# Two fewer plain pairs in FFNs 2 to 4 of a float32 decoder trunk on one Trainium2 core

## The reference, cut to what matters

```python
def modulate(x, g, shift, scale):
    return rmsnorm(x, g) * (1.0 + scale[:, None, :]) + shift[:, None, :]

def swiglu(h, w13, w2):
    gate, up = jnp.split(h @ w13, 2, axis=-1)
    return (jax.nn.silu(gate) * up) @ w2
...
        h = modulate(x, norm_g[i, 0], ada[:, 0, 0], ada[:, 0, 1])
        x = x + 0.5 * ada[:, 0, 2, None, :] * swiglu(h, ffn_w13[i, 0], ffn_w2[i, 0])
        ... (mixer 0: mLSTM, mixer 1: differential attention)
        h = modulate(x, norm_g[i, 2], ada[:, 2, 0], ada[:, 2, 1])
        x = x + 0.5 * ada[:, 2, 2, None, :] * swiglu(h, ffn_w13[i, 1], ffn_w2[i, 1])
```

## Time and profile before

| | |
|---|---|
| median of 3 runs | 1879.09 us (1878.94 to 1879.1) |
| the profiled execution, device time | 1878.92 us |
| its span in the trace | 1877.1 us |
| PE busy | 1858.1 us, 99% of the span |
| PE weight loads | 1679.9 us, 89% |
| DVE busy | 1457.2 us, 78% |
| ACT busy | 890.2 us, 47% |
| POOL busy | 41.5 us, 2% |
| DMA | 270.87 MB, 144 GB/s on average |

### The profile page before, as it was taken

The page is one execution under the profiler, slowest core; times in us unless marked ns, Lnnn a source line. Parts: engine busy times, 40 slices in busy tenths (PEclk is TensorE's granted clock), DMA queues, the critical chain, the costliest instruction groups (busy, mean ns, idle before and its releaser), DMA issues. The chain is left out here.

```text
span 1877.1 us, 30566 instructions
## 1 busy us (share of the span) xinstructions
PE 1858.1 (99%) x11872; PEld 1679.9 (89%) x11872; DVE 1457.2 (78%) x2041; ACT 890.2 (47%) x1414; POOL 41.5 (2%) x36
## 2 busy tenths in 40 slices
PE   8999999999999999999999999999999999999998
PEld 6999988888779999998899999889877799999887
DVE  7899978785678888878688887886787778888433
ACT  6566632344334656642255655224344555656322
POOL 4000000000000100000010000000000010000000
PEclk9999999999999999999999999999999999999999
DMA  8344369624113422359643232972321243322432
GB/s 316 120 161 163 110 242 332 237 92 157 57 46 124 135 104 98 112 215 334 212 146 106 108 112 87 349 246 82 113 68 45 72 131 113 112 100 96 138 99 83
DMA packets 84115, 270.87 MB, mean 144 GB/s; under 512 B 8593, under 2 KB 16913, under 8 KB 83258
## 3 DMA queue, kind: packets, MB, share of 16 engines
q1 hardware_dynamic: 83616, 267.62, 41.5%
q0 software_dynamic: 352, 2.11, 0.3%
q10 hardware_dynamic: 58, 0.00, 0.0%
HBM read 261.30 MB, written 8.40 MB: 144 GB/s over the span
## 5 line engine op out<-in xcount | busy, mean ns | idle before, releaser
L698 PE MATMUL acc<-h_hi,w_hi 128*128 128x256 f32 (+1 forms) x1178 | 378.6, 321 | 4.1 <-DVE w_lo L1765 1.2
L1975 DVE TENSOR_TENSOR w_lo<-arena,w_hi 128x1024 fp32r<-128x1024 f32 (+1 forms) x288 | 307.5, 1088 | 95.7 <-ACT w_hi L1333 92.8
L1256 ACT ACTIVATE w_hi<-arena 128x1024 fp32r<-128x1024 f32 (+2 forms) x223 | 201.4, 904 | 369.0 <-DMA arena<-w 174.3
L700 PE MATMUL acc<-h_hi,w_lo 128*128 128x256 f32 (+1 forms) x1178 | 369.8, 314 | 0.0
L699 PE MATMUL acc<-h_lo,w_hi 128*128 128x256 f32 (+1 forms) x1178 | 369.7, 314 | 0.0
L1765 DVE TENSOR_TENSOR w_lo<-arena,w_hi 128x768 fp32r<-128x768 f32 (+1 forms) x220 | 226.7, 1032 | 145.6 <-ACT w_hi L1256 144.0
L1333 ACT ACTIVATE w_hi<-arena 128x1024 fp32r<-128x1024 f32 (+1 forms) x288 | 272.9, 949 | 79.9 <-PE stats L700 30.8
L698 PE MATMUL outp<-g_hi,w_hi 128*128 128x512 f32 (+1 forms) x792 | 290.3, 367 | 0.0
L699 PE MATMUL outp<-g_lo,w_hi 128*128 128x512 f32 (+1 forms) x792 | 289.5, 365 | 0.0
L700 PE MATMUL outp<-g_hi,w_lo 128*128 128x512 f32 (+1 forms) x792 | 289.4, 365 | 0.0
L698 PEld LDWEIGHTS acc<-h_hi,w_hi 128*128 128x128 f32 x1178 | 224.5, 191 | 24.0 <-issue 3.6
(11 more groups left out here) (319 smaller groups left out, 3521.4 us busy)
## 6 DMA issues: line engine op xcount, KB each, us to landing
arena<-w SPq DMA_DIRECT2D x174, 512.0 KB, 4.4
arena<-ada SPq DMA_DIRECT2D x58, 512.0 KB, 5.8
ada_raw<-ada SPq DMA_DIRECT2D x57, 512.0 KB, 5.7
arena<-w SPq DMA_DIRECT2D x64, 384.0 KB, 3.6
arena<-w SPq DMA_DIRECT2D x64, 320.0 KB, 4.3
arena<-wa SPq DMA_DIRECT2D x33, 512.0 KB, 3.6
arena<-wb SPq DMA_DIRECT2D x32, 512.0 KB, 3.5
early_ada<-ada SPq DMA_DIRECT2D x8, 1024.0 KB, 17.6
```

The lines of the kernel that those rows point to most:

```text
L698: pe.matmul(bank, a_hi, b_hi, start=start, stop=False, skip_group_check=onto)
L700: return pe.matmul(bank, a_lo, b_hi, start=False, stop=stop, skip_group_check=onto)
L1256: act.activation(w_hi[base % SLOTS][:, 0:n], src[:, 0:n], ACT.Copy).then_inc(hi_ready, 1)
L1975: dve.tensor_tensor(slot(w_lo[s], n), two_factors(j, n), slot(w_hi[s], n).bitcast(F32), ALU.subtract)\
```

## The change

FFN 1 stays as it is. In FFNs 2 to 4 only two pairs are plain (the first group), and 20 are fast.

- The four plain units of 512 tokens go, on every engine. So the first fast pair follows the first group directly.
- The left sums of the first two fast pairs are not made by DVE. SP loads blocks of their raw weights into a new tile `soon` (5 transfers a pair, `load_soon`), at the upper end of the memory of `g_lo`, once `unit_done` says that the last unit ahead of this FFN is through. POOL then issues 4 accumulating transfers a pair (`soon_sum`), which add further blocks of the same weights from HBM onto `soon`. The first two of a pair are independent, the third waits for those, the fourth for the third.
- The right sums start from the tiles without the shift. T1 is a difference in which the shift cancels: DVE makes it inside the norm's second half. T3 and T2 are 4 instructions each of 128x256 with the shift (or the difference of shifts, `shift_gap`) as the scalar. T4 needs one quarter of the input with its shift; ACT adds that in the norm, 4 instructions of 128x256 ahead of `root(n, 1)`. `full_modulated` and `whole` go.
- `store_x` of both halves stands behind the 10 loads into `soon` in SP's queue; that of the second half no longer waits for the modulated input but for `sq_added`.
- The orders of ACT and DVE for the first fast pair are new (`fast_soon`), and PE takes the right factors in the order T3, T2, T1, T4.

```diff
-PLAIN = (4, 4, 4, 4)
+PLAIN = (4, 2, 2, 2)
...
                 def store_x(half):
-                    sp.wait_ge(src_ready, Q_IN[n] + KT * (half + 1))
+                    if half:
+                        sp.wait_ge(sq_added, ADD_BASE[n - 1] + 1 + SQUARES[n - 1])
+                    else:
+                        sp.wait_ge(src_ready, Q_IN[n] + KT)
                     sp.dma_start(x_copy[:, :, tok(half)], x[:, :, tok(half)]).then_inc(x_stored, 16)
+                def load_soon(j):
+                    sp.wait_ge(unit_done, U_FFN[p])
+                    gate, up = [w13[p * N13 + 2 * (PLAIN[p] + j) + part] for part in range(2)]
+                    for first, last, src in ((0, 2, up), (2, 4, gate), (4, 5, up[:, 0:512]), (5, 6, gate[:, 0:512]), (6, 8, gate)):
+                        sp.dma_start(soon[:, j, first:last, :].rearrange("p a s -> p (a s)"), src)                          .then_inc(soon_loaded[j], 16)
...
+                    for j in range(SOON):
+                        load_soon(j)
                     store_x(0)
-                    load13(p, 4)
-                    load13(p, 5)
                     store_x(1)
-                    load13(p, 6)
-                    load13(p, 7)
...
+            def soon_sum(p, j, n):
+                up, gate = [w13[p * N13 + 2 * (PLAIN[p] + j) + part] for part in (1, 0)]
+                first, last, src = ((4, 5, up[:, 512:1024]), (5, 8, up[:, 0:512]), (6, 8, up[:, 512:1024]),
+                                    (7, 8, gate[:, 0:512]))[n]
+                if n == 0:
+                    pool.wait_ge(soon_loaded[j], SOON_LOADS * 16 * p)
+                elif n > 1:
+                    pool.wait_ge(soon_added[j], 16 * (4 * (p - 1) + n))
+                pool.dma_start(soon[:, j, first:last, :], src.unsqueeze(1).broadcast_to([P, last - first, 512]),
+                               accum_op=ALU.add).then_inc(soon_added[j], 16)
             for p in range(1, 4):
-                for k in range(KT // 2, KT):
-                    whole(p, k)
+                for j in range(SOON):
+                    soon_sum(p, j, 0)
+                    soon_sum(p, j, 1)
+                for n in (2, 3):
+                    for j in range(SOON):
+                        soon_sum(p, j, n)
...
+                if n in N_FFN:
+                    for k in range(KT // 2, KT):
+                        act.wait_ge(act_lo_ready, Q_IN[n] + k + 1)
+                        act.activation(mod[:, k, tok(0)], mod[:, k, tok(0)], ACT.Identity,
+                                       bias=ada_v[:, 3 * n, k:k + 1]).then_inc(whole_ready, 1)
                 root(n, 1)
...
-                    act.wait_ge(sums_ready, 3 * (F + j) + (1, 2, 1, 3)[n])
+                    if p and j < SOON:
+                        act.wait_ge(soon_added[j], 16 * (4 * (p - 1) + (2, 3, 2, 4)[n]))
...
+                    if n in N_FFN and half and k == KT // 2 + 1:
+                        dve.wait_ge(src_ready, Q_IN[n] + KT + KT // 2)
+                        dve.tensor_tensor(right_sum(T1), right_sum(T1), right_sum(T3), ALU.subtract)\
+                           .then_inc(t_summed, 1)
```

More of the change, by code:

```diff
@@ L64 @@
 UNITS_B = 16 + 8 + 8
-PLAIN = (4, 4, 4, 4)
+PLAIN = (4, 2, 2, 2)
 FAST = tuple(FT - n for n in PLAIN)
 FAST_SLOTS = 4
+SOON = 2
+SOON_LOADS = 5
+PAIR_LOADS = tuple((n - (SOON if p else 0)) // 2 for p, n in enumerate(FAST))
 UNITS = tuple(2 * n + FAST_SLOTS * m + NW2 for n, m in zip(PLAIN, FAST))
@@ L85 @@
 FAST_BEFORE = tuple(sum(FAST[:p]) for p in range(4))
-HALF_BEFORE = tuple(n // 2 for n in FAST_BEFORE)
+HALF_BEFORE = tuple(sum(PAIR_LOADS[:p]) for p in range(4))
 def loads(base):
-    return base // RAWS - sum(FAST_SLOTS * FAST[p] // RAWS - FAST[p] // 2 for p in range(4) if base >= W_FFN[p])
+    return base // RAWS - sum(FAST_SLOTS * FAST[p] // RAWS - PAIR_LOADS[p] for p in range(4) if base >= W_FFN[p])
 def more_uses(before, *uses):
@@ L349, in build_trunk @@
         t_summed = sem("t_summed")
+        gap_ready = sem("gap_ready")
+        soon_loaded = [sem(f"soon_loaded{i}") for i in range(SOON)]
+        soon_added = [sem(f"soon_added{i}") for i in range(SOON)]
         t_hi_ready = sem("t_hi_ready")
@@ L505, in fast_raw, with two_factors @@
             return (1, 0) if j % 2 == 0 else (3, 2)
-        def two_factors(j, r):
+        def two_factors(p, j, r):
+            if p and j < SOON:
+                a, b = ((2, 5), (3, 6), (1, 4), (7, 7))[r]
+                return soon[:, j, a:b + 1:b - a, :] if a < b else soon[:, j, 7, :]
             gate, up = fast_raw(j)
@@ L582, in ffn_fast @@
                         load13(p, i)
+                    for j in range(SOON):
+                        load_soon(j)
                     store_x(0)
[L584 to L585 removed]
                     store_x(1)
[L587 to L589 removed]
+                for j in range(SOON if p else 0, FAST[p]):
                     load_pair(j)
@@ L1330, in factor_high @@
                         return
-                    act.wait_ge(sums_ready, 3 * (F + j) + (1, 2, 1, 3)[n])
+                    if p and j < SOON:
+                        act.wait_ge(soon_added[j], 16 * (4 * (p - 1) + (2, 3, 2, 4)[n]))
+                    else:
+                        act.wait_ge(sums_ready, 3 * (F + j - SOON * p) + (1, 2, 1, 3)[n])
                     act.wait_ge(unit_done, B + FAST_SLOTS * j + n - SLOTS + 1)
-                    act.activation(slot(w_hi[(B + n) % SLOTS], n), two_factors(j, n), ACT.Copy).then_inc(hi_ready, 1)
+                    act.activation(slot(w_hi[(B + n) % SLOTS], n), two_factors(p, j, n), ACT.Copy).then_inc(hi_ready, 1)
                 def tap(j, n):
@@ new lines, in fast_soon @@
+                def fast_soon():
+                    right_high(0)
+                    act.preload_act_table(ACT.Silu)
+                    factor_high(0, 0)
+                    right_high(1)
+                    right_high(2)
+                    factor_high(0, 1)
+                    gate_of(p, 0)
+                    factor_high(0, 2)
+                    tap(0, 0)
+                    right_high(3)
+                    factor_high(0, 3)
+                    gate_of(p, 1)
+                    tap(0, 1)
+                    factor_high(1, 0)
+                    factor_high(1, 1)
+                    tap(0, 2)
+                    keep_shared(0)
+                    product_high(p, 0)
+                    product_high(p, 1)
+                    factor_high(1, 2)
@@ L1376, in fast_pairs @@
+                if p:
+                    fast_soon()
+                else:
+                    plain_then_fast()
+                for j in range(1 if p else 0, FAST[p]):
                     if j:
```

154 lines of the change are left out of this document (95 added, 59 removed).

## The result

The changed kernel takes 1952.95 us (median of 4 runs, 1950.3 to 1955.24); the kernel before, beside it, 1879.01 (4 runs, 1878.24 to 1879.1). The ratio is 1.0396, 95% interval 1.0383 to 1.0409. The prediction had the sign, with 1890.2, but its range ended at 1904.0: the cost came out nearly seven times as large as forecast, +73.9 us against +11.1.

The account below looks back on a forecast made before the run. PE, busy 99%, was taken as the bound: 1878.92 - 4.9 (PE's gain) + 13.3 (late stores) + 2.4 (steps behind the start) + 0.3 (FFN 3's root) = 1890.0, as median 1890.2; range 1874.7 to 1904.0.

Parts of the forecast that it names:

- What bounds the kernel, and PE's gain of 4.9 us: PE, busy 99%, sets the pace; two fast pairs replacing four plain units gain 1.63 us in each of three FFNs.
- all covered: Rival: POOL's adds take only what SP's queue leaves, x is stored by 612.3, PE does not wait; 1875.0, chance 0.24.
- The stores of x, 13.3 us: Ahead of T1's high part ACT waits for late stores of x: stalls of 4.9, 3.5 and 4.9 us in FFNs 2 to 4.
- In at 611.9 with nothing beside them: FFN 2: without POOL's transfers beside them, both stores of x land at 611.9, just in time for 612.3.
- the 5.3 us for POOL's transfers: FFN 2: delay of the stores by POOL's adds, 3.5 us for pair 0's and half of it for pair 1's.
- The further adds of pair 0 are taken as in time: Pair 0's later adds, the third due about 1.9 us after factor 0's copy, were assumed in time in the sum.
- must have done so before ACT's first factor: POOL adds pair 0's first two pieces, 1.05 MB, once loads land (about 600.5), and must finish before ACT's first factor.
- adds at twice the price: Rival: adding transfers cost twice the forecast's price and hold up the stores of x; 1905.9, chance 0.18.
- The steps behind the start, 2.4 us: ACT and DVE in lockstep just ahead of PE in the first fast pair: 0.8 us an FFN (0 to 4 in all).
- What would show it: Profile signs: PE gap before the first fast pair, ACT waiting for stored x; wrong if ACT waits for `soon` instead.

Follow-up runs that it names:

- The plain copies: Changed kernel with POOL's transfers into `soon` copying instead of adding, so these left sums are left out: 1898.06 us.
- the kernel with 2304: Changed kernel with `dynamic_dma_scratch_size` 2304 instead of 1024, and the identity in place of the two causal masks: 1924.09 us.
- the run with POOL's sums: Changed kernel with the first two pairs' left sums made by POOL's own adder from two loaded blocks a pair, without adding transfers: 1893.71 us.

## Why the prediction had the sign and not the size

- **What bounds the kernel, and PE's gain of 4.9 us.** Right: without adds and without late stores the time is 1874.0 beside a forecast of 1875.0 for "all covered", and the gain of 3.0 to 6.6 us holds the 4.9. The pace of the fast pairs did not change: in the changed kernel the gates stand at 673.89 and 683.97, again 10.08 us apart.
- **The stores of x, 13.3 us.** ACT's wait was there, 4.41, 3.30 and 4.67 us against 4.9, 3.5 and 4.9. That it came out so near was luck, for two errors cancelled in it. "In at 611.9 with nothing beside them" was 4.0 us too early, for I counted only what stands ahead of the stores in SP's queue and not the loads behind them that ran beside. And the 5.3 us for POOL's transfers were 0 in FFN 2 and 1.9 and 1.4 in the others, since POOL had moved only 0.30 MB by 616. The plain copies show 4.3 us for traffic that does get out. Nor was this term what made the kernel slower: it lay under the wait for the adds, and the sign came out right over another wait than the one forecast.
- **"The further adds of pair 0 are taken as in time".** This step failed, and with it the one before, that POOL's first two adds "must have done so before ACT's first factor". ACT waited 65.8 us for `soon` in 8 waits, in FFN 2 3.74, 15.30 and 3.11, where the sum has nothing; behind these PE lost the whole 66.6 us. The runs showed POOL waiting at its issue in place of transfers in time: the third add was issued at 634.03, 17.5 us after its factor was due. I had the due time of the third add (about 1.9 us after factor 0) and no issue time for it. By the change it was the fifth of eight transfers in one queue, four of them chained behind others. The third add follows two others that must have landed. At 4.8 to 9.4 us for a landing that chain of two takes 10 to 19 us from 600.5, where the factor wanted it at about 616.5, 16 us later: in doubt by my own rows, even before the queue. The prediction never made that sum.
- **The rival "adds at twice the price".** It got 0.18 and 1905.9, by an estimate that took twice the 3.0 us of the earlier trace rows for an add. No row of the kernel before shows that price, on which the upper end of the range, 1904.0, rested too. The runs showed it, 5.9 to 6.3 us for each MB against 2.8, but not its reason. The case that the rival had in view was that of the kernel with 2304. Even there it was too small: PE waited 45.5 us for the stores' sake, where it had 27.7, and nothing for the third add, where it had 1.3 an FFN; measured 1924.09. In the changed kernel it was the other way round, with little delay of the stores and 13.67 us of PE in FFN 2 for the third add.
- **POOL's wait at its issue.** Not in any case of the prediction. It cost about 29 us. The kernel before has no adding transfer and only four transfers of POOL's, so no row showed it; the 1024 stands in the code, and I did not ask what it would mean for eight transfers in a row.
- **The clock.** The sum had stalls only. PE's waits of 7 and 14 us were followed by stretches at a granted clock of 0.50 to 0.73, about 12 us in all. The same happened behind shorter ones: 0.72, 0.50, 0.75 from 605 to 620 in the run with POOL's sums, where PE's longest wait was 3.4 us.
- **The steps behind the start, 2.4 us.** Near 0: PE's waits there come to 0.6 us in the run without adds and with the stores between the loads.
- **What would show it.** The last sentence named it: ACT waiting for `soon` would mean that the adds are late. It was priced at nothing all the same.

## What to carry to other kernels

Work moved from an engine to transfers gets a due time for each transfer, and the queue's whole pace is set against them: number of transfers in a row times the time between issues, chain by chain, not bytes by a rate. A price worked out from what stands ahead in a queue also has to hold what the queue issues behind it: here 7.75 MB moved where I had counted 6.29. When a term rests on one wait, ask which wait would be next: here the first could be removed at no gain, because a longer one lay beneath.

## What the runs showed of the hardware

- Adding transfers from POOL's queue used 5.9 to 6.3 us of the 16 engines for each MB, and 5760 packets for 11.0 MB; the same bytes copied, 2.8 us and 3072 packets.
- With `dynamic_dma_scratch_size` at 1024 POOL sat 3.6 to 10.1 us at the issue of the next adding transfer in FFN 2; with 2304 it never did.
- With 2304, the adds filled the engines (a DMA share of 1.11 at 231 GB/s), and SP's stores of 1 MB landed in 24.1 us (median), against 12.6 in the same order without adds, 16.4 beside plain copies and 5.1 in the kernel before. With 1024 the adds, issued later, cost ACT 0, 1.9 and 1.4 us of waiting for the stores in the three FFNs.
- POOL's sum of 128x1024 and DVE's `h_lo` step excluded each other (0.49 us became 2.56); beside DVE's reciprocal POOL's sum of 128x512 took 1.29 us and the reciprocal 1.75, as without it.
